# Two-part modulation sums, reordered mixers in the second block, and nine taps ahead of head statistics in a four-layer transformer kernel

## What is computed

```python
# first block, per layer
mod = silu(c) @ ada_w[l] + ada_b[l]           # 9 vectors of 1024: shift, scale, gate for three sub-layers
h = h + 0.5*g1 * swiglu(rms(h)*(1+sc1)+sh1)
z = (rms(h)*(1+sc2)+sh2) @ w_in[l]
mixed = [differential attention, 31-tap causal conv + layernorm + swish,
         chunked spatial gating, forgetting attention (logits + cumulative log f)]
h = h + g2 * (mixed @ w_out[l])
h = h + 0.5*g3 * swiglu(rms(h)*(1+sc3)+sh3)
# second block, per layer: swiglu, then
k, log_f = (1-lb)*sigmoid(-z), logaddexp(log lb, log1p(-lb)+log_sigmoid(z))   # HGRN2 recurrence, 8 levels here
mixed = sigmoid(ga)*(hgrn @ Wb1) + sigmoid(gb)*(window attention with sinks @ Wb2)
x = x + rms(mixed @ w_out); then swiglu again
```

## Time and profile before

| | |
|---|---|
| median of 3 runs | 2337.99 us (2335.66 to 2340.73) |
| profiled execution, its time | 2339.15 us |
| its span, first to last instruction | 2337.4 us |
| PE busy | 2261.6 us, 97% of the span |
| DVE, ACT, POOL busy | 1608.4, 1128.8, 99.4 us |
| mean granted TensorE clock | 0.980 of full |
| memory read | 449.92 MB, 193 GB/s over the span |

### The profile page before, as it was taken

One profiled execution on the slowest core, in us unless ns is written; L12 is line 12 of the kernel. 1 busy time (PEld: TensorE's weight loads), 2 busy tenths in 40 slices (PEclk: granted clock), 3 DMA queues, 4 the chain that ended last, 5 costly groups with the idle time before them and its releaser, 6 DMA issues.

```text
span 2337.4 us, 31813 instructions
## 1 busy us (share of the span) xinstructions
PE 2261.6 (97%) x11791; PEld 1904.5 (81%) x11801; DVE 1608.4 (69%) x1843; ACT 1128.8 (48%) x1312; POOL 99.4 (4%) x145
## 2 busy tenths in 40 slices
PE   7999999999999999999999999999999998999998
PEld 6887877887788787788788789988878888998887
DVE  6876886876776687766665667675566556857555
ACT  4344554444444455544444474654454447565433
POOL 1000031000000103000000000000000000000000
PEclk8999988999999999999999999999999999999999
DMA  9985533886688453566565554356556555334653
GB/s 321 338 309 183 173 121 131 305 309 222 209 286 269 153 181 126 168 219 217 169 198 183 176 150 139 109 196 197 181 175 203 183 189 150 127 109 162 205 190 108
DMA packets 323522, 452.24 MB, mean 193 GB/s; under 512 B 31590, under 2 KB 269032, under 8 KB 323432
## 3 DMA queue, kind: packets, MB, share of 16 engines
q1 hardware_dynamic: 320456, 440.98, 57.4%
q0 software_dynamic: 2704, 8.99, 1.1%
q10 hardware_dynamic: 272, 1.05, 0.1%
HBM read 449.92 MB, written 1.05 MB: 193 GB/s over the span
## 4 chain that ended last, share of the span: by engine, by line
PE 86%; DVE 8%; ACT 3%; issue 2%; DMA 0%; POOL 0%; SPq 0%; DVEq 0%; ACTq 0%
PE ps L598 20%; PE ps L600 20%; PE ps L599 20%; PE ps L591 4%; PE ps L592 4%; PE ps L593 4%; DVE wlo L1909 2%; PE ps L761 1%; PE ps L1158 1%; PE ps L910 1%; PE ps L743 1%; PE ps L744 1%; PE ps L746 1%; PE ps L688 1%; PE ps L1018 1%
## 5 line engine op out<-in xcount | busy, mean ns | idle before, releaser
L1909 DVE TENSOR_TENSOR wlo<-raw,whi 128x2048 fp32r<-128x2048 f32 (+1 forms) x348 | 791.6, 2278 | 352.5 <-ACT whi L1299 349.2
L1299 ACT ACTIVATE whi<-raw 128x2048 fp32r<-128x2048 f32 x346 | 660.0, 1910 | 293.1 <-PE ps L600 238.9
L598 PE MATMUL ps<-whi,xl 128*128 128x512 f32 x1472 | 591.5, 402 | 0.0
L600 PE MATMUL ps<-whi,xh 128*128 128x512 f32 x1472 | 574.1, 390 | 0.0
L599 PE MATMUL ps<-wlo,xh 128*128 128x512 f32 x1472 | 573.9, 390 | 0.0
L598 PEld LDWEIGHTS ps<-whi,xl 128*128 128x128 f32 x1472 | 276.6, 188 | 61.2 <-issue 4.3
L600 PEld LDWEIGHTS ps<-whi,xh 128*128 128x128 f32 x1472 | 276.4, 188 | 59.9
L599 PEld LDWEIGHTS ps<-wlo,xh 128*128 128x128 f32 x1472 | 276.8, 188 | 58.3 <-issue 4.3
L591 PE MATMUL ps<-xl,whi 128*128 128x256 f32 x864 | 251.6, 291 | 7.6 <-DVE wlo L1909 7.6
L598 PE MATMUL ps<-whi,hidl 128*128 128x512 f32 x640 | 251.9, 394 | 0.0
L600 PE MATMUL ps<-whi,hidh 128*128 128x512 f32 x640 | 249.2, 389 | 0.0
(11 more groups left out here) (406 smaller groups left out, 2551.7 us busy)
## 6 DMA issues: line engine op xcount, KB each, us to landing
raw<-in_ffn_w_in_dram SPq DMA_DIRECT2D x176, 512.0 KB
arena<-in_ada_w_dram SPq DMA_DIRECT2D x144, 512.0 KB, 6.0
raw<-in_w_in_dram SPq DMA_DIRECT2D x54, 1024.0 KB
raw<-in_ffn_w_out_dram SPq DMA_DIRECT2D x44, 1024.0 KB
raw<-in_w_ffn_gate_dram SPq DMA_DIRECT2D x88, 512.0 KB
raw<-in_w_ffn_up_dram SPq DMA_DIRECT2D x88, 512.0 KB
raw<-in_w_ffn_down_dram SPq DMA_DIRECT2D x44, 1024.0 KB
raw<-in_w_out_dram SPq DMA_DIRECT2D x16, 1024.0 KB
```

The source lines that it names most:

```text
L598: pe.matmul(o, al, wh, start=start, stop=False, **kw)
L600: return pe.matmul(o, ah, wh, start=False, stop=stop, **kw)
L1299: act.activation(whi[:, k % 3, :], raw[:, k % 3, :], ACT.Copy).then_inc(hi_done, 1)
L1909: tt(a[0], a[1], a[2].bitcast(F32), ALU.subtract).then_inc(lo_done, 1)
```

## The change

1. `ones_row` becomes fp32r. Each of the 32 sums is now made of two fp32r matmuls: ACT copies 512 columns of `acc` (rounded) to `upper_row`, DVE subtracts it into `lower_row`, PE adds both. `upper_row` and `lower_row` have one buffer each, so each upper part waits until the sum before it is done.
2. In the first block's mixer tail, the sums move: sum 0 from ahead of the conv mean to behind `project(0,1)`, the others one place later each. In the same tail DVE gets `lower_sum(0)` ahead of `craw`, `lower_sum(1)` behind `lo(k0+14)`, `lower_sum(2)` and `(3)` ahead of `summed(2)` and `(3)`; ACT gets `upper_sum(0)` behind `turned_out`, and `hi(k0+14)` goes ahead of `summed(0)`.
3. `taps(9, 18)` goes ahead of `head_stat(L,1,..)`.
4. Second block's mixer: both abs go from ACT to DVE (as max(x, -x), signal `habs`), `lo(k0+6)` goes ahead of the forget-gate arithmetic, the first `logits` goes behind `decayed(5)`, `take(3)`, `spans(6)`; PE does z(13) ahead of `turn(L,0,SA)`; ACT does `decay(8)` and the copy of z(13) ahead of `turned_out`; half of the newton step goes ahead of `rest_out(2)`.
5. `gcum` and `sel` go; the forget-gate sums lie in the unused rows of z's `f`, and columns of the identity replace `sel`. `wmask` shares `amask`. The arena shrinks by 1028 columns, the size of the two new rows.

```diff
@@ tensor
+                pe.wait_ge(acc_lower, parts_summed(m, q) + 1)
                 pe.wait_ge(mod_read, SUMS[m] + q)
-                pe.matmul(ps[:, sumb(m), :], ones_row[:, :], acc[:, 512 * q:512 * q + 512], start=True,
-                          stop=True).then_inc(mod_summed, 1)
+                pe.matmul(ps[:, sumb(m), :], ones_row[:, :], lower_row[:, :], start=True, stop=False)
+                pe.matmul(ps[:, sumb(m), :], ones_row[:, :], upper_row[:, :], start=False, stop=True).then_inc(mod_summed, 1)
...
+                z(13)
                 turn(L, 0, SA)
-                z(13)
...
+                taps(9, 18)
                 head_stat(L, 1, 1, blk64, sq8, [ps[:, 6, :], ps[:, 7, :]])
-                taps(9, 18)
...
                 pe.wait_ge(z_copied[0], l * NZ[0] + 11)
-                modulation(m, 0)
...
                 project(0, 1).then_inc(unit_used, 1)
+                modulation(m, 0)
+                project(1, 1).then_inc(unit_used, 1)
                 modulation(m, 1)
-                project(1, 1).then_inc(unit_used, 1)
-                modulation(m, 2)
                 pe.wait_ge(s["o"], seq(L, OUTS, 3))
                 project(2, 0)
+                modulation(m, 2)
+                project(2, 1).then_inc(unit_used, 1)
                 modulation(m, 3)
-                project(2, 1).then_inc(unit_used, 1)
@@ scalar
+            def upper_sum(m, q):
+                if q == 0:
+                    act.wait_ge(adam_used, ADAM[m + 1] + 2)
+                else:
+                    act.wait_ge(mod_summed, SUMS[m] + q)
+                act.activation(upper_row[:, :], acc[:, 512 * q:512 * q + 512], ACT.Copy).then_inc(acc_upper, 1)
@@ feed-forward
+                    upper_sum(m, 0)
                 hi(L, k + 4)
                     summed(m, 0)
+                    upper_sum(m, 1)
                     summed(m, 1)
+                    upper_sum(m, 2)
                 upper(g)
                 hi(L, k + 5)
                 sigmoid(g + 1, 0)
+                    upper_sum(m, 3)
                 sigmoid(g + 1, 1, k + 3)
+                    upper_sum(m, 4)
                 hi(L, k + 6)
                     summed(m, 4)
+                    upper_sum(m, 5)
                     summed(m, 5)
+                    upper_gate(n, 0)
                 hi(L, k + 7)
                     gate0(n, 0)
+                    upper_gate(n, 1)
                     gate0(n, 1)
@@ second block's mixer
+                hi(L, k0 + 6)
+                act.wait_ge(s["habs"], 2 * l + 1)
                 st(act.activation(u8h[0], u8h[0], ACT.Exp, scale=-1.0))
                 act.activation(u8h[0], u8h[0], ACT.Ln, bias=ones_col[:, 0:1]).then_inc(s["hz4"], 1)
-                hi(L, k0 + 6)
+                copy(4)
+                hi(L, k0 + 7)
                 act.wait_ge(s["hz1"], l + 1)
@@ first block's mixer tail
                 turned_out(L, 1, PT1)
+                upper_sum(m, 0)
                 act.wait_ge(s["craw"], l + 1)
...
+                hi(L, k0 + 14)
                 summed(m, 0)
-                hi(L, k0 + 14)
-                summed(m, 1)
+                upper_sum(m, 1)
                 act.wait_ge(s["cy"], 2 * l + 1)
                 act.activation(zt["cg"], zt["ca"], ACT.Sigmoid).then_inc(s["cexp"], 1)
+                summed(m, 1)
+                upper_sum(m, 2)
                 act.wait_ge(s["cy"], 2 * l + 2)
                 act.activation(xo(2, 4), zt["ca"], ACT.Copy).then_inc(s["outh"], 1)
+                upper_sum(m, 3)
                 hi(L, k0 + 15)
@@ vector
+            def lower_sum(m, q):
+                dve.wait_ge(acc_upper, parts_summed(m, q) + 1)
+                tt(lower_row[:, :], acc[:, 512 * q:512 * q + 512], upper_row[:, :].bitcast(F32), ALU.subtract).then_inc(acc_lower, 1)
@@ feed-forward
+                sums(0)
                 lo(L, k + 4)
+                sums(1, 2)
                 lower(g)
                 lo(L, k + 5)
                 product(g + 1, 0)
                     summed(m, 2)
+                sums(3)
                 product(g + 1, 1)
                     summed(m, 3)
+                sums(4)
                 lo(L, k + 6)
+                sums(5)
+                    lower_gate(n, 0)
                 lo(L, k + 7)
+                    lower_gate(n, 1)
@@ second block's mixer
+                copied(L, 3)
+                stt(u8h[0], hf, -1.0, hf, ALU.mult, ALU.max).then_inc(s["habs"], 1)
+                lo(L, k0 + 6)
...
-                lo(L, k0 + 6)
+                dve.wait_ge(s["hz3"], l + 1)
+                stt(sq8h[0], sq8h[0], -1.0, sq8h[0], ALU.mult, ALU.max).then_inc(s["habs"], 1)
                 lo(L, k0 + 7)
...
                 lo(L, k0 + 12)
-                logits(L, st, 0, SA, wmask, 0.125, 0)
                 decayed(5)
                 take(L, 3)
                 spans(6)
+                logits(L, st, 0, SA, wmask, 0.125, 0)
                 lo(L, k0 + 13)
@@ first block's mixer tail
                 lo(L, k0 + 13)
+                lower_sum(m, 0)
                 dve.wait_ge(s["cmean"], l + 1)
...
                 lo(L, k0 + 14)
+                lower_sum(m, 1)
                 dve.wait_ge(s["cexp"], l + 1)
                 tt(zt["ca"], zt["ca"], zt["cg"], ALU.mult).then_inc(s["cy"], 1)
                 rest_out(L, 4, 2, 4, zt["ca"])
+                lower_sum(m, 2)
                 summed(m, 2)
+                lower_sum(m, 3)
                 summed(m, 3)
                 lo(L, k0 + 15)
```

More of the change, by code:

```diff
@@ L119, in program @@
         lnr = sb("lnr", [P, 4, 2])
-        ARENA = 14912
+        upper_row = sb("upper_row", [P, 512], F32R)
+        lower_row = sb("lower_row", [P, 512], F32R)
+        ARENA = 13884
         arena = sb("arena", [P, ARENA])
@@ L186, in program @@
         AT = c2(12, P)
-        wmask = c2(384)
+        wmask = amask
         dist = c2(384)
@@ L239, in program @@
                      "gmixed", "cmean", "cvar_sq", "cexp", "cy", "dout", "craw",
-                     "sq", "convrest", "convsum", "lam", "sigm", "silu", "hz", "hz1", "hz2", "hz3", "hz4", "ld", "le", "lx", "lmm", "sunk", "esink",
+                     "sq", "convrest", "convsum", "habs", "hroot", "lam", "sigm", "silu", "hz", "hz1", "hz2", "hz3", "hz4", "ld", "le", "lx", "lmm", "sunk", "esink",
                      "hpv", "hsq", "gates", "branch", "mixed", "mixh", "hcum", "taken", "hgs", "hfin", "att_read")
@@ L584, in program, with parts_summed @@
         SUMS = (0, 4, 10, 14, 20, 26, 30)
+        def parts_summed(m, q):
+            return SUMS[m] - 4 + q
         @block.tensor
@@ L918, in scores @@
                             o, keys = out_of[qb](h), P * (qb + 1)
-                            pe.matmul(o, gcum[0:4, 0, qb * P:qb * P + P], sel[0:4, h, 0:1].to_broadcast([4, keys]), start=False,
+                            pe.matmul(o, gsum[0:4, qb * P:qb * P + P], ident[0:4, h:h + 1].to_broadcast([4, keys]), start=False,
                                       stop=True, skip_group_check=True)
-                            last = pe.matmul(o, sel[0:4, h, 0:P], gcum[0:4, 1, 0:keys], start=False, stop=True,
+                            last = pe.matmul(o, ident[0:4, h:h + 1].to_broadcast([4, P]), gneg[0:4, 0:keys], start=False, stop=True,
                                              skip_group_check=True)
@@ L1480, in ffn @@
                 k = k0 + 3 * g
+                if m:
+                    upper_sum(m, 0)
                 hi(L, k + 4)
@@ L1589, in mix1 @@
                 ins.then_inc(s["hz2"], 1)
-                copy(4)
-                hi(L, k0 + 7)
-                act.wait_ge(s["hz3"], l + 1)
-                st(act.activation(sq8h[0], sq8h[0], ACT.Abs))
+                act.wait_ge(s["habs"], 2 * l + 2)
                 st(act.activation(sq8h[0], sq8h[0], ACT.Exp, scale=-1.0))
@@ L1621, in mix1 @@
                 hi(L, k0 + 15)
-                turned_out(L, 0, PTA)
                 decay(8)
                 copy(13)
+                turned_out(L, 0, PTA)
                 hi(L, k0 + 16)
@@ L2078, in ada_gate, with lower_gate, sums @@
                 stt(accg, adag, condT[:, 0, bass.ds(k, 1)], accg, ALU.mult, ALU.add).then_inc(adag_used, 1)
+            def lower_sum(m, q):
+                dve.wait_ge(acc_upper, parts_summed(m, q) + 1)
+                tt(lower_row[:, :], acc[:, 512 * q:512 * q + 512], upper_row[:, :].bitcast(F32), ALU.subtract).then_inc(acc_lower, 1)
+            def lower_gate(n, q):
+                dve.wait_ge(gate_upper, 2 * GATED.index(n) + q + 1)
+                tt(lower_row[:, :], accg[:, 512 * q:512 * q + 512], upper_row[:, :].bitcast(F32), ALU.subtract).then_inc(gate_lower, 1)
             def ffn(L, n, j, k0):
                 g0, h0, m = L.ffn(j) * GROUPS, L.ffn(j) * (GROUPS - 1), (n + 1 if n < 5 else 0)
+                def sums(*qs):
+                    for q in qs if m else ():
+                        lower_sum(m, q)
                 def product(g, a):
```

57 lines of the change are left out of this document (35 added, 22 removed).

## The result

| | before | after |
|---|---|---|
| median of 20 runs each | 2338.18 us | 2344.07 us |
| lowest and highest | 2332.59, 2343.55 | 2331.63, 2354.93 |
| standard deviation of the runs | 2.7 us | 7.4 us |
| ratio, 95% interval | | 1.0029, 1.0017 to 1.0042 |
| profiled execution: time, span, granted clock | 2339.15, 2337.4 us, 0.980 | 2344.89, 2343.1 us, 0.981 |

I forecast 2334 us, with a range of 2323 to 2343. It came out 10 us longer than that, one above the range, and on the slower side, to which I had given 0.16.

A forecast was written before the change was run, and what follows sets the result against it. TensorE was taken to bound the kernel, with 86% of the chain that ended last. The terms -3.2 + 8.1 + 2.4 + 0 - 5.6 - 4.2 - 1.7 = -4.2 took 2337.99 to about 2334 us, range 2323 to 2343.

The forecast's parts named there:

- the slower side: Whole kernel: slower than before by more than a measurement can tell, about 0.2% or 4.7 us; chance 0.16.
- Nine taps ahead of the head statistics: First block's mixers: taps fill TensorE's 1.78 us wait, next statistics' chain does not move; 0, between -2 and +2 us.
- The tail: End of first block's mixers: TensorE waits 3.45 us at sum 1, next boundary 4.05 us later each; +8.1 us.
- The clock: First block's mixers: half-clock stretch behind the new 3.45 us wait, charged 1.2 us in each; +2.4 us.
- third rival: First block's mixers and second block's attention: further half-clock stretches follow waits, including at the boundary; 2345 us, chance 0.14.
- The sums in the feed-forwards: Sub-layers 0, 2, 3, 5: two fp32r matmuls save 0.40 us per sum, less a wait at sum 3; -3.2 us together.
- The second block's mixers: Sub-layers 7 and 10: gates -5.6 us, attention -4.2 us, and -1.7 us for a half-clock stretch gone in sub-layer 10.
- the attention part: Second block's mixers: z(13) fills the 3.1 us wait, -2.1 us each, plus -1.7 us of clock in sub-layer 10.
- the gates: Second block's mixers: z(6) starts without its 2.53 us wait and abs on DVE ends earlier; -2.8 us each, -5.6 us.
- second rival: Second block's attention: waits only shift to `level(5)` and `turned_out`, no gain there or in clock; 2340 us, chance 0.20.

The follow-up runs named there:

- the combination with the tail reordered once more: Against the kernel before: second block's mixers and all two-part sums as changed, taps in their old place, first-block tail links moved earlier on ScalarE and VectorE; ratio 0.9942.

## Why the prediction was wrong

**The step that failed is "Nine taps ahead of the head statistics", costed at 0 between -2 and +2: it took the chain to the next statistics for one that does not move.** It measured +6.8 us alone (3.5 to 9.8) and 8.2 by taking it out of the whole. I had the wait of 1.78 us right, which nine taps of 0.43 would overfill, and then wrote that "little is late", since ScalarE was in a softmax and a table load until 321.8, and that the next statistics wait for a chain "that does not move". Three things were wrong with it, in the order of the trace:

- The table load is not cover for the statistics. It stands behind them: 2.08 and 4.83 us of ScalarE's wait end with L950, and only then come the 1.28 of the load. The cover was the softmax alone.
- The diagonals cost 1.35 and 2.41 us in the changed kernel, 0.6 and 2.41 with the taps alone, where I had said 0.7. GpSimd's diagonal took 2.40 us in the one mixer, beside `lo(k0+11)`, an instruction of VectorE that reads two tiles of SBUF, and 3.54 in the other, beside most of an `ada` and the whole `lo`, against 0.37 for one that runs alone (rows behind this list). I had seen the contention in the earlier trace rows, took its mean of 0.82, and did not ask which single diagonal TensorE would stand behind. The taps were moved to just where that one is. (The GPSIMD Engine Reference of the Trainium skill, Specifications, names the contention with VectorE's instructions that have two SBUF inputs; the trace agrees.)
- The chain does move. It begins with that table load. In the 24 mixers of the profiles without the nine taps the load follows the softmax at once (once with 0.27 us between). Counted from the sub-layer's start it comes 1.2 and 4.6 us later than before in the profile with the taps alone, and 0.5 and 4.7 later in the changed kernel; the next statistics come 1.2 and 4.4, and 0.5 and 4.4 later. What the load is late, they are late.

How this makes up the 6.8 us is clear only in part. In the mean over the 24 mixers the last `turn` before the tail stands 135.0 us into the sub-layer, and 138.1 in the mean over the four with the nine taps: 3.1 us a mixer, 6.2 for the two. But this holds half clock too. With the taps alone sub-layer 1 has one stretch of 3.4 us at half clock fewer than before (27.3 us against 30.7) and sub-layer 4 two more (23.9 against 17.1), one of them behind the wait for the diagonal. At 1.7 us a stretch, an estimate from these lengths, the delay itself is 1.3 and 2.8 us. No run has the nine taps with their diagonals ready, which would part the taps from the wait for the diagonal.

GpSimd's timeline of the changed kernel, one diagonal alone, and in each mixer the two ahead of TensorE's wait, of which the second is the one held up:

```profile
308.55 0.37 POOL L2698 TENSOR_SCALAR side<-ident,prm 128x128 f32<-128x128 f32 x1 [0.48 <-PE ps L1162]
...
318.24 3.79 POOL L2698 TENSOR_SCALAR side<-ident,prm 128x128 f32<-128x128 f32 x2 [4.41 <-PE ps L1162]
...
884.17 4.85 POOL L2698 TENSOR_SCALAR side<-ident,prm 128x128 f32<-128x128 f32 x2 [5.82 <-PE ps L1162]
```

Four taps, as long as the idle time, bring no loss (-2.8 to +1.9 us), which is the same statement from the other side.

**The tail: right.** Forecast 5.25 us each with its clock, measured 5.15 each, in the whole change (31.84 and 31.83 us against 26.69 and 26.68) and alone. The wait stands where it was put, behind `lo(k0+14)`. **The clock: right in the tails, short by the boundary.** In all six tails with the 3 us wait a stretch of 3.4 us at half clock follows, in the two with 1.8 us none. I had left the third rival's stretch at the boundary out; with the mixers' sums alone it costs 1.3 and 1.1 in the sub-layers behind, and in the change 1.25 in sub-layer 2, which is why that shows -0.2 for -1.5 (198.14 us in the run of the feed-forwards' sums alone, 199.39 here). The length of the wait alone does not decide it: in sub-layer 7 the wait of 3.10 us at L929 has none behind it in the kernel before, and one of 3.4 us in the profile with the mixers' sums alone, at the same code (before, then mixers' sums):

```profile
1450.30:1453.70 3.40, 3.40 (x31) 3.40 (x30) 3.40 (x4) 2.41 (x3) 0.00 (x0) 1.00 0.57 197
1460.40:1463.80 3.40, 3.40 (x18) 3.40 (x18) 3.40 (x5) 0.87 (x1) 0.00 (x0) 0.51 0.70 244
```

(By the Trainium skill, TensorE: Matmul & The Clock Gate, "Why this matters for your kernels", a long enough pause between bursts of matmuls sends the engine to half rate. Here the 3 us waits of the tails do so each time and the 1.8 us ones do not, but the 3.10 us one did so only in some executions.)

**The sums in the feed-forwards: right** in the profiles, within 0.2 in each (sum 3 waits 1.4 us for `lower_row` in sub-layer 3, as forecast); the runs neither show a gain nor reach the forecast -3.2.

**The second block's mixers: right**, -11.2 for the -11.5 forecast, of which the attention part -6.3 for -5.9 and the gates -4.7 for -5.6. That the waits would only shift (second rival) did not come about, though one did: the 1.2 us at `take`.

**The sum again**, with what the runs gave for each part alone: -11.2 +0.0 +12.6 +6.8 = +8.2 us; as a product of ratios 1.0035, inside the 1.0017 to 1.0042 of the change. My own sum of -4.2 with the taps at +6.8 and the boundaries at +2.4 would have been +5.0, where the medians differ by 5.9. In the changed kernel's profile the boundaries cost 1.25, not 2.4.

**What stays open.** The standard deviation is 7.4 us for the changed kernel, 2.7 for the one before, 4.4 for the taps alone, and 2.4 for the change without the taps: both kernels with the nine taps scatter more, and why was not tested. Over the 20 runs time and granted clock go together (correlation -0.81): the eight at a mean clock of 0.978 or less take 2344 to 2355 us, the nine at 0.982 or more 2332 to 2344. So a long run is one with more half clock. Which of the stretches come and go from run to run was not seen, for only one run of it has a profile.

## What to carry to other kernels

- Before work is put into an idle gap of one engine, ask what the instruction behind the gap heads. Here it headed a chain over ScalarE and VectorE to the next meeting: work as long as the gap was free, twice as much cost some 3 us a mixer in the mean. Whether a table load is part of the chain or cover for it is read from its row: this one began only after the statistics, but the load at L1729 of the kernel before ran while its activation was still to wait for VectorE:

```profile
892.36 1.28 ACT L1729 ACT_TABLE_LOAD   x1
894.68 0.63 ACT L1729 ACTIVATE arena<-arena 128x512 f32<-128x512 f32 x1 [1.03 <-DVE arena L2420]
```

- A link over two engines costs what stands in their lists ahead of it, not its own length: the same eight instructions cost 5.15 (1.7 of it half clock), 1.8 or 0.45 us a tail, by order alone.
- In a change of several parts, test the parts: two of the four here were worth -13 us together (-11.2 of it the second block's), and the two others ate them up.

## What the runs showed of the hardware

The same code takes different times by where stretches at half clock fall. The first block's mixer, with neither its taps nor its sums changed, took 157.82 us in sub-layer 1 and 164.28 in sub-layer 4 of one execution (the feed-forwards' sums alone), with mean clocks of 0.95 and 0.92:

```profile
235.44:393.26 157.82, 149.64 (x897) 126.88 (x898) 126.19 (x172) 88.11 (x133) 35.18 (x49) 0.95 0.46 151
788.15:952.43 164.28, 155.11 (x898) 129.83 (x898) 126.39 (x172) 88.06 (x133) 32.80 (x47) 0.92 0.45 145
```

It held 17 us at half clock in the one case and 27 in the other. When all stretches fell alike, as in the combination with the tail reordered once more, its two mixers took 164.92 and 164.91 us (0.45 of each for the two-part sums). So a difference of under 7 us in one such sub-layer of one profile says nothing by itself; the distance between two marks that no changing stretch lies between (the tail, 26.66 to 26.71 us in all 18 with float32 sums) tells hundredths.
